# Rows ahead of the value weights' splits, spatial weights loaded and turned later, small vectors behind the gates' inputs

## What is computed

```python
cond = silu(c) @ ada_w + ada_b                 # 6 vectors of 1024: shift1, scale1, gate1, ...
h = rmsnorm(x, norm1_g) * (1 + scale1) + shift1
z = h @ w_in + b_in                            # 1024 x 2048
u, v, val, gate = split(z, 4)                  # 512 columns each
# spatial gating of u and v: v is normed over channels, then mixed over 128 positions
v = layernorm(gelu(v)); v = tril(w_s) @ v + b_s       # 8 heads, each 128 x 128
y_a = gelu(u) * v
# conformer: value and gate, then 31 taps over the positions, each channel by itself
y = depthwise_conv31(val * sigmoid(gate))
```

## Time and profile before

| | |
|---|---|
| time, median of 3 runs | 762.83 us |
| time, lowest and highest | 761.18, 768.16 us |
| span of the profiled execution | 769.1 us |
| mean granted TensorE clock | 0.954 |
| PE busy | 92% |
| DVE, ACT, POOL busy | 47%, 42%, 8% |
| HBM read | 209.51 MB, 274 GB/s over the span |

### The profile page before, as it was taken

One profiled execution on the slowest core, in us unless ns is written; L12 is line 12 of the kernel. 1 busy time (PEld: TensorE's weight loads), 2 busy tenths in 40 slices (PEclk: granted clock), 3 DMA queues, 4 the chain that ended last, 5 costly groups with the idle time before them and its releaser, 6 DMA issues.

```text
span 769.1 us, 13134 instructions
## 1 busy us (share of the span) xinstructions
PE 709.7 (92%) x5455; PEld 561.9 (73%) x5456; DVE 361.4 (47%) x718; ACT 325.2 (42%) x690; POOL 61.2 (8%) x72
## 2 busy tenths in 40 slices
PE   4889999999999999999999999997999999879786
PEld 2685768887999999999988777876875555344352
DVE  2459967447545555444579589444431111111011
ACT  2365734726444443334566895857321111001011
POOL 0400002000000002000000028162000000000000
PEclk9899999989999999999898999999989999989997
DMA  9998979409667644455453346568869999999996
GB/s 335 354 404 336 370 290 334 157 23 375 218 238 240 222 164 166 169 176 164 164 198 132 124 141 196 164 219 356 308 271 422 421 421 419 420 421 419 421 408 216
DMA packets 75683, 211.44 MB, mean 275 GB/s; under 512 B 7463, under 2 KB 34245, under 8 KB 61798
## 3 DMA queue, kind: packets, MB, share of 16 engines
q1 hardware_dynamic: 74578, 209.91, 72.4%
q0 software_dynamic: 800, 0.63, 0.5%
q10 hardware_dynamic: 244, 0.03, 0.0%
HBM read 209.51 MB, written 1.05 MB: 274 GB/s over the span
## 4 chain that ended last, share of the span: by engine, by line
PE 65%; DMA 13%; DVE 10%; ACT 6%; SPq 3%; issue 2%; ACTq 0%; DVEq 0%
PE ps L1974 10%; PE ps L1975 9%; PE ps L1976 9%; PE ps L2699 6%; PE ps L1987 4%; PE ps L1988 4%; PE ps L1989 4%; DMA ring<-in_expert_w_up_dram 4%; DMA ring<-in_expert_w_gate_dram 4%; DVE YT L1341 3%; DVE ring_low L1225 3%; DMA Z<-in_expert_w_up_dram 3%; SPq L457 3%; PE ps L2668 3%; PE ps L2741 3%; DMA ring<-in_w_in_dram 2%
## 5 line engine op out<-in xcount | busy, mean ns | idle before, releaser
L1225 DVE TENSOR_TENSOR ring_low<-ring,HI 128x1024 fp32r<-128x1024 f32 (+1 forms) x119 | 142.0, 1236 | 27.0 <-ACT HI L712 26.9
L712 ACT ACTIVATE HI<-ring 128x1024 fp32r<-128x1024 f32 (+1 forms) x135 | 133.5, 1055 | 29.0 <-DMA ring<-in_w_in_dram 29.0
L1974 PE MATMUL ps<-AH,HI 128*128 128x256 f32 x320 | 90.1, 282 | 0.3 <-DVE Z L1492 0.3
L1976 PE MATMUL ps<-AH,ring_low 128*128 128x256 f32 x320 | 89.6, 280 | 0.0
L1975 PE MATMUL ps<-AL,HI 128*128 128x256 f32 x320 | 89.5, 280 | 0.0
L2699 PE MATMUL ps<-ring,ZM 128*32 128x256 f32 x880 | 72.7, 421 | 13.7 <-DMA ring<-in_expert_w_up_dram 10.7
L1974 PE MATMUL ps<-HI,AH 128*128 128x512 f32 (+1 forms) x176 | 71.7, 407 | 2.0 <-DVE ring_low L1225 1.0
L1975 PE MATMUL ps<-ring_low,AH 128*128 128x512 f32 (+1 forms) x176 | 69.1, 392 | 0.0
L2699 PEld LDWEIGHTS ps<-ring,ZM 128*32 128x32 f32 x880 | 34.6, 120 | 41.2 <-DMA ring<-in_expert_w_up_dram 14.1
L1987 PE MATMUL ps<-AH,HI 128*128 128x256 f32 x192 | 57.7, 301 | 7.3 <-DVE AL L1311 5.7
L1976 PE MATMUL ps<-HI,AL 128*128 128x512 f32 (+1 forms) x160 | 62.6, 391 | 0.0
(11 more groups left out here) (394 smaller groups left out, 1293.6 us busy)
## 6 DMA issues: line engine op xcount, KB each, us to landing
ring<-in_expert_w_up_dram SPq DMA_DIRECT2D x28, 1024.0 KB, 24.7
ring<-in_expert_w_gate_dram SPq DMA_DIRECT2D x27, 1024.0 KB, 26.2
ring<-in_expert_w_down_dram SPq DMA_DIRECT2D x24, 1024.0 KB, 23.9
ring<-in_w_ffn_in_dram SPq DMA_DIRECT2D x20, 1024.0 KB, 6.5
ring<-in_w_in_dram SPq DMA_DIRECT2D x18, 1024.0 KB, 6.0
ring<-in_ada_w_dram SPq DMA_DIRECT2D x16, 1024.0 KB, 9.1
ring<-in_w_ffn_out_dram SPq DMA_DIRECT2D x11, 1024.0 KB, 7.1
ring<-in_ada_w_dram SPq DMA_DIRECT2D x16, 512.0 KB, 11.1
```

What stands on the lines that cost most here:

```text
L712: act(HI[:, (i + 1) % UNITS, 0:w], W.view(name)[:, o:o + w], ACT.Copy).then_inc(s_hi, 1)
L1225: tt(W.low(name)[:, o:o + w], W.view(name)[:, o:o + w], HI[:, (i + 1) % UNITS, 0:w].bitcast(F32), ALU.subtract).then_inc(s_lo, 1)
L1974: mm(dst, lh, rh, start=start, stop=False)
L1976: return mm(dst, ll, rh, start=False, stop=stop)
```

## The change

- **SP's queue.** The spatial weights' transfer (0.5 MB in 512-byte pieces) goes from ahead of in_v1 to behind in_u0. The `ada` chunks 2 and 3 of the second set go ahead of the wait for s_rp at 3.
- **POOL.** The 17 small transfers wait for s_ada at 8, not 4.
- **Second half's rows.** PE turns the vector (`columns_half(1)`) behind the first of four channel tiles of in_g0's second unit, not behind the whole unit. ACT no longer splits u4 and u5 ahead of the rows: AH 4 and 5, then u4, then AH 6 and 7, then u5. DVE likewise does u4 behind the second pair of rows' scaling, not ahead of the first.
- **Small vectors.** PE turns them (L2160, L2161) behind in_g1, not ahead of in_v1. DVE copies them (L1320, L1321) behind the splits of u8 and u9.
- **Spatial matrices.** PE turns them in two groups of four, behind the `ada` products of v's first unit and behind the diagonals of the second, both in bank 6; ACT copies each group out. The sums follow behind the third unit's diagonals. DVE's four instructions for E go from ahead of u12's split to behind u14's.
- **ACT in v's strip.** The squares of the memory go from ahead of u13's split to behind u13's split and the second group of diagonals.

```diff
@@ sync
             ada_half(1, (2, 3))
-            const(wsv, A["a_spatial_w"]..., s_ws)
             rows128("in_v1", w_in, 1024, 512, 4, 4)
             rows128("in_g1", w_in, 1536, 512, 4, 4)
             sp.dma_start(brow_v, A["b_in"][:, 512:1024]).then_inc(*W.other(BROW))
             rows128("in_u0", w_in, 512, 512, 0, 4)
+            const(wsv, A["a_spatial_w"]..., s_ws)
             ada(A["ada_w"], 1, (0, 1), 2048)
             rows128("in_u1", w_in, 512, 512, 4, 4)
+            ada(A["ada_w"], 1, (2, 3), 2048)
             sp.wait_ge(s_rp, 3)
             ...
-            ada(A["ada_w"], 1, (2, 3), 2048)
@@ gpsimd
-            po.wait_ge(s_ada, 4)
+            po.wait_ge(s_ada, 8)
@@ scalar
-                hi_to((0, 5)[h])
+                if h == 0:
+                    hi_to(0)
             ...
-                        hi_to(4 * h + 1)
+                        hi_to((1, 4)[h])
             ...
-            for hh in range(2):
-                ac.wait_ge(s_wtp, hh + 1)
-                act(WT[:, 4 * hh:4 * hh + 4, :], ps[4 + hh]..., ACT.Copy).then_inc(s_wt, 1)
             ...
             diagonals(0)
+            spatial_turned(0)
             hi_to(iu + 1 + AHEAD)
+            spatial_turned(1)
+            hi_to(iu + 2 + AHEAD)
+            diagonals(1)
             ac.wait_ge(s_mem, 32)
             ...
-            hi_to(iu + 2 + AHEAD)
-            diagonals(1)
@@ vector
-                if h:
-                    lo_to(4)
             ...
+                    if k0 == 6:
+                        lo_to(4)
             ...
+            lo_to(S.first["in_u0"] + 1)
             ve.wait_ge(s_rp, 3)
             copy(C2[:, 0:ROWS2], ps[6][:, P:P + ROWS2]).then_inc(s_rc, 1)
             copy(cw[:, :, 0:TAPS], ...).then_inc(s_rc, 1)
-            lo_to(S.first["in_u0"] + 1)
             ...
@@ tensor
+            def inside_second(q, ct):
+                if q == 1 and ct == 0:
+                    columns_half(1)
+            by_channel(("in_g0",), gate, "gate", (), between_second, 0, inside_second)
+            by_channel(("in_v1",), value, "value", (), lambda q: None, 2)
+            by_channel(("in_g1",), gate, "gate", (), lambda q: None, 2)
             te.wait_ge(s_r2, 16 * LOADS2)
             tr(ps[6][:, 0:4 * TAPS], rowsc...).then_inc(s_rp, 1)
             tr(ps[6][:, P:P + ROWS2], rows2...).then_inc(s_rp, 1)
             ...
+                if i < 2:
+                    spatial_turned(i)
+                if i == 2:
+                    spatial_sums()
```

More of the change, by code:

```diff
@@ L501, in _ @@
             rows128("in_u0", w_in, 512, 512, 0, 4)
+            const(wsv, A["a_spatial_w"].rearrange("o h t s -> t (o h) s"), s_ws)
             ada(A["ada_w"], 1, (0, 1), 2048)
             rows128("in_u1", w_in, 512, 512, 4, 4)
+            ada(A["ada_w"], 1, (2, 3), 2048)
             sp.wait_ge(s_rp, 3)
@@ L781, in _ @@
             hi_to(7)
-            for hh in range(2):
-                ac.wait_ge(s_wtp, hh + 1)
-                act(WT[:, 4 * hh:4 * hh + 4, :], ps[4 + hh][:, :].rearrange("p (h s) -> p h s", h=4),
-                    ACT.Copy).then_inc(s_wt, 1)
             hi_to(S.first["in_u0"] + 1)
@@ L804, in diagonals, with spatial_turned @@
                     act(DM[:, j % 8, :], ident[:, :], ACT.Copy, scale=cw[:, 3, j:j + 1]).then_inc(s_dm, 1)
+            def spatial_turned(hh):
+                ac.wait_ge(s_wtp, hh + 1)
+                act(WT[:, 4 * hh:4 * hh + 4, :], ps[6][:, :].rearrange("p (h s) -> p h s", h=4), ACT.Copy).then_inc(s_wt, 1)
             hi_to(iu + AHEAD)
@@ L1346, in _ @@
             taps(2, 4)
[L1348 to L1353, removed]
             lo_to(iu + 1 + AHEAD)
@@ L1361, in _ @@
             lo_to(iu + 3 + AHEAD)
+            ve.wait_ge(s_wtp, 3)
+            ve.wait_ge(s_rc, 2)
+            ve.wait_ge(s_un, S.first["in_u0"] + 1)
+            for ct in range(4):
+                stt(E[:, ct, :], ps[6][:, P * ct:P * ct + P], C2[:, LNB + ct:LNB + ct + 1], BSb[:, ct, :], ALU.mult,
+                    ALU.add).then_inc(s_e, 1)
             taps(13, 17)
@@ L2116, in _, with by_channel @@
             columns_half(0)
-            def by_channel(names, place, n, starts, between, q0=0):
+            def by_channel(names, place, n, starts, between, q0=0, inside=None):
                 us = [u for x in names for u in range(S.first[x], S.end[x])]
@@ L2131, in by_channel @@
                             ins.then_inc(s_glu, 1)
+                        if inside is not None:
+                            inside(q, ct)
                     ins.then_inc(s_un, 1)
@@ L2161, in _, with spatial_turned, spatial_sums @@
             tr(ps[6][:, P:P + ROWS2], rows2[0:ROWS2, :], ident[0:ROWS2, 0:ROWS2]).then_inc(s_rp, 1)
-            te.wait_ge(s_set, MASKED)
-            te.wait_ge(s_xc, 8)
-            te.wait_ge(s_rc, 1)
-            for hh in range(2):
+            def spatial_turned(hh):
+                if hh == 0:
+                    te.wait_ge(s_set, MASKED)
+                    te.wait_ge(s_rc, 3)
+                else:
+                    te.wait_ge(s_wt, 1)
                 for h in range(4):
-                    ins = tr(ps[4 + hh][:, h * P:(h + 1) * P], wsv[:, 4 * hh + h, :], ident[:, :])
+                    ins = tr(ps[6][:, h * P:(h + 1) * P], wsv[:, 4 * hh + h, :], ident[:, :])
                 ins.then_inc(s_wtp, 1)
-            by_channel(("in_v1",), value, "value", (), lambda q: None, 2)
-            by_channel(("in_g1",), gate, "gate", (), lambda q: None, 2)
-            te.wait_ge(s_wt, 2)
-            te.wait_ge(s_rc, 3)
-            for h in range(8):
-                ins = mm(ps[6][64 * (h % 2):64 * (h % 2) + 64, P * (h // 2):P * (h // 2) + P], ones[:, 0:64], WT[:, h, :],
-                         start=True, stop=True)
-            ins.then_inc(s_wtp, 1)
+            def spatial_sums():
+                te.wait_ge(s_wt, 2)
+                for h in range(8):
+                    ins = mm(ps[6][64 * (h % 2):64 * (h % 2) + 64, P * (h // 2):P * (h // 2) + P], ones[:, 0:64], WT[:, h, :],
+                             start=True, stop=True)
+                ins.then_inc(s_wtp, 1)
             def diagonals(i):
```

5 lines of the change are left out of this document (2 added, 3 removed).

## The result

The changed kernel takes 771.21 us, the median of 19 runs (769.76 to 777.53). The kernel before, run beside it, takes 763.85 us (19 runs, 760.61 to 773.56). The ratio is 1.0118 with a 95% interval of 1.0091 to 1.0146: the change costs 9.0 us, between 7.0 and 11.2, where 3.5 were forecast. The ratio leaves out executions that are more than 1.5% above the fastest of their kernel, which are the six slowest of the kernel before and none of the changed one; over all 19 against 19 the medians differ by 7.36 us.

A forecast was written before the change was run, and what follows sets the result against it. DMA engines bound it up to 60 us, PE and DVE from 65 to 89, then DVE's copy of the vector. That copy, 2.6 to 4.2 us late, taken as 3.5, gave 762.83 + 3.5 = 766.3 us; range 760.5 to 771.

The forecast's parts named there:

- The second half's start: PE's start of in_v1: at 42.3 us instead of 44.76, a gain of 2.4 us.
- In_g1's end: PE's end of in_g1, four units after in_v1's start: at 53.8 us instead of 56.2.
- The small vectors: POOL's later transfers: landed at 52.6 us, PE wants them at 53.8, so no cost, with 1.2 us cover.
- v's strip and ACT: PE turns the second spatial group at 68.6 to 70.2 us; ACT's squares are done at 74.6 to 76.2, against 68.42.
- DVE: DVE waits 1.9 to 3.5 us for the squares; its copy comes at 92.4 to 94.0 us, 2.6 to 4.2 late.
- The wait for u12: A new DVE wait at u12's split, which waits for in_w0: 3 us, from 62.6 to 65.65 us.
- a shift at 90 us is a shift at the end, one for one: Behind DVE's copy of the vector: any delay there passes on unchanged to the kernel's end.
- The gain: Rival: DVE never stands between 60 and 76 us, so the 2.4 us stay; 760.4 to 763 us, chance 0.16.
- The vectors: Rival: POOL's issues are slowed and PE waits 7.9 us at 53.8; up to 774.2 us, chance 0.08.
- The clock case: Rival: TensorE's clock falls in PE's 6 us wait for the copy, 1.6 us a spell; 767.9 to 769.5, chance 0.24.

The follow-up runs named there:

- rows_undone: The changed kernel with the second half's rows back in their old order, loads, vectors and v's strip staying changed; 1.0102 of the kernel before.
- squares_first: The changed kernel with ACT's squares of the memory put back ahead of the second spatial group's copy, u13 and the diagonals; 1.0071 of the kernel before.
- sum_late: The changed kernel with DVE's wait for the squares and their sum moved behind taps 8 to 12, u14's split and E; 1.0096 of the kernel before.
- taps_first: sum_e_late with DVE's splits of u12 and u13 moved behind taps 4 to 7 and 8 to 12; 0.9996 of the kernel before.
- taps_filler: taps_first with two unused float32 products of 128x512 on PE ahead of in_v1; 1.0002 of the kernel before.
- sum_e_late: sum_late with E's four DVE instructions also moved behind the copy of the vector; 1.0055 of the kernel before.

## Why the prediction was wrong

**The second half's start: right in size, wrong in its cause.** 42.3 was forecast and 42.18 came. I had put the gain down to the rows, with the loads as its condition; rows_undone shows the same start without the rows' move.

**In_g1's end: 53.8 forecast, 55.12 measured.** The low clock that was in v's strip came at 43.5 to 47 us instead. Where it did not, as in rows_undone, the vectors were turned at 53.75, in the forecast place. The small vectors cost PE nothing, as forecast. DVE's copies of them, which had an idle stretch of 4.17 us behind them, now stand right ahead of its first taps (55.52 to 56.03, some 0.5 us), a term that I left out and that its wait for u12 covered here. POOL now issues them beside DVE's rows and splits:

```profile
37.49 0.71 POOL L617 DMA_DIRECT2D KM<-in_b_conv_w_dram  x1 [35.53 <-PE ps L2068]
38.20 0.54 POOL L617 DMA_DIRECT2D KM<-in_ada_b_dram  x1
...
45.98 0.58 POOL L617 DMA_DIRECT2D gcol<-in_ffn_norm_dram  x1
```

The seventeen take until 46.56, 9.1 us as before, and the last of them, with its 7.0 us to landing, is in at 53.0. The Trainium skill (SBUF — State Buffer, the box on the trap in which DVE blocks DMA) has GpSimd locked out while DVE runs a two-port operation. No issue here shows that: they took 0.50 to 0.58 us each, first and stack of two apart, beside DVE's work. From issue to landing it was 5.6 to 7.0 us, where it was 4.9 to 6.5 before; why is not shown.

**v's strip and ACT: right.** The second group was forecast for 68.6 to 70.2 and was turned at 69.61; the squares for 74.6 to 76.2 and were done at 76.0. u12's split did not move.

**DVE: right, at the upper end.** Forecast were the sum at 74.6 to 76.2 and the copy at 92.4 to 94.0; it was 76.16 and 93.92. From sum to copy it took 17.76 us, the 16.72 and the 1.04 of E. I took 3.5 us of a range of 2.6 to 4.2, and 4.13 came. The wait for u12 was 1.33 us and not 3, as v's strip began 1.4 us later than forecast (57.33 against 55.9) and the 0.5 us of copies stood ahead of the taps. squares_first and sum_late show in their traces that this wait, and the second group ahead of it, is the cause.

**The step that failed: "a shift at 90 us is a shift at the end, one for one".** Two terms are missing in the sum.
- The clock falls in PE's new stand. I had seen that and made it a rival with 0.24, since 2.95 us at 1.00 spoke against it. Four kernels, the changed one among them, stood for 3.58 us or more at this place, and from copy to ML they took 21.62 to 22.80 us; the other nine traces have a stand of at most 1.65 us and took 19.82 to 19.84. The term is 1.79 us. The rival's own price, 1.6 us a spell, was good. By the Trainium skill (TensorE: Matmul & The Clock Gate, "What's actually happening") an idle engine falls back to half rate; the trace agrees at this place, with 0.54 at 91 to 98 us.
- Behind ML another 1.43 us are lost. From ML to the product nine traces take 83.68 to 83.87 us, early ones (taps_first) and late ones alike, and taps_filler 85.27; only sum_e_late, whose ML is 0.3 us from the kernel before, keeps 82.3, as both traces of before do. I had no case for this.

With them the account closes: 762.83 was forecast from, 763.85 is the median of 19 runs (1.0); 4.13 instead of 3.5 (0.6); 1.8; 1.4. Together 4.9, and 771.21 less 766.3 is 4.9; with medians this uncertain the last tenths agree by luck. The 1.43 us go with the clock. The stretch from ML to the product, in the kernel before and in the changed one:

```profile
109.62:191.92 82.30, 77.83 (x606) 66.80 (x604) 52.18 (x97) 45.76 (x79) 4.09 (x7) 0.96 0.64 222
115.54:199.27 83.73, 79.25 (x606) 68.06 (x604) 52.20 (x98) 45.77 (x79) 4.11 (x7) 0.94 0.61 216
```

In all thirteen traces the length follows the granted clock: 0.96 in the three that take 82.3 us, 0.94 in the nine that take 83.7 to 83.9, 0.92 in taps_filler with its 85.27. No run takes a fall away there alone, so that the fall is the cause is argued from this; why it is longer in some kernels stays open.

**The rivals.** The gain did not come through, since DVE waited in both places. The vectors were not late. The clock case was the one that came true; with the second loss it passed its own price by 1.7 us (769.5 against 771.21) and the range by 0.2.

**What the tail does.** From the first expert product to the end it is 200.8 to 201.1 us in all thirteen traces, so nothing is won or lost there; in between, the stretch from the product to the first expert product took 376.1 us in the profiled execution of before and 367.9 in that of after, and 366.3 to 376.1 over all thirteen. This is why the shorter span belongs to the slower kernel. 192 to 568 us has the clock at 0.97 before and at 1.00 after, in the fences above. That this stretch is alike in the median executions of the two kernels is assumed in the account above and not shown; sum_e_late, whose time doesn't fit its product, is a warning.

## What to carry to other kernels

Before a step is hung behind another engine, count what it carries with it: here the squares of a matrix that nobody was waiting for in ACT's queue held DVE, and DVE held the one copy that PE needed. When the sum shows that PE will stand for several microseconds where it didn't before, the low clock after the stand may belong into the sum, and not among the rivals; a few products for nothing, which wait for nothing, are a quick test of that. And where the executions of a kernel come in groups, one trace's span says little: compare the same instruction in both traces, and more than one trace of each kernel.

## What was not expected of the hardware

- **The times come in groups, and the slower group has the lower mean clock.** The kernel before in the last of its rounds: 14 of 23 executions between 761.1 and 765.6 us with a mean granted clock of 0.965 to 0.975, and 9 between 770.9 and 774.1 us with 0.950 to 0.966. It is the same program each time. By the traces such a difference can arise behind the product: that stretch takes 366.3 us where its clock is 1.00 (sum_late, taps_first) and 376.1 where it is 0.97 (before, sum_e_late).
- **A stand of 2.95 us was followed by no fall, one of 3.58 us was.** Between the two nothing was measured, and a stand of 1.78 us ahead of in_v1 was followed by a fall in the changed kernel, and by none in sum_late (42.40), so the length of the stand alone doesn't decide it.
- **A fall at the copy cost 1.8 to 3.0 us.** In the changed kernel, where 91 to 98 us are at 0.54 and PE stood idle until 94.66, it was 1.8 us. In the other three kernels with a fall it was 2.2 to 3.0 us.
- **Seven unused products of 512 columns, 6.17 us of PE, cost nothing** in front of a copy that was late, and gave 1.79 us back in the trace.
